# Layer input kept on chip between layers, with its squares summed in the output projection; paired heads in retention; a spare bank for the queries' sums

## What is computed

```python
def trunk_layer(x, c, pos, hist, norm_w, ada_w, ada_b, w_in, ...):
    mod = jax.nn.silu(c) @ ada_w + ada_b
    shift, scale, gate = jnp.split(mod[:, None, :], 3, axis=-1)
    h = rmsnorm(x, norm_w) * (1.0 + scale) + shift
    proj = h @ w_in                                  # 16 parts: q, k, v, gates of three branches
    ...
    o_ret = rmsnorm(o_r, ret_norm_w.reshape(H_RET, DV_RET)).reshape(B, S, BRANCH_W) * jax.nn.silu(rz)
    ...                                              # o_fox, o_gdn likewise
    q_g = l2norm(q_g.reshape(B, S, H_GDN, DK_GDN)) * (DK_GDN ** -0.5)
    br = jnp.einsum('bsnc,ncd->bsnd', jnp.stack([o_ret, o_fox, o_gdn], axis=2), w_branch)
    out = jnp.sum(br * jax.nn.sigmoid(mg), axis=2) @ w_out
    return x + gate * out, new_state
# after both layers: y = rmsnorm(x, final_norm_w)
```

## Time and profile before

| | |
|---|---|
| time, median of 3 runs | 3134.73 us (3130.49 to 3139.78) |
| the profiled execution's own time | 3135.03 us |
| span from its first to its last instruction | 3133.3 us |
| mean granted TensorE clock | 0.981 |
| TensorE busy | 2964.6 us, 95% |
| VectorE, ScalarE, GpSimd busy | 44%, 32%, 28% |
| traffic | 278.18 MB, 89 GB/s |

### The profile page before, as it was taken

The page is one execution under the profiler, slowest core; times in us unless marked ns, Lnnn a source line. Parts: engine busy times, 40 slices in busy tenths (PEclk is TensorE's granted clock), DMA queues, the critical chain, the costliest instruction groups (busy, mean ns, idle before and its releaser), DMA issues. The chain is left out here.

```text
span 3133.3 us, 52349 instructions
## 1 busy us (share of the span) xinstructions
PE 2964.6 (95%) x22200; PEld 2741.3 (87%) x22200; DVE 1365.4 (44%) x2813; ACT 997.5 (32%) x1798; POOL 890.0 (28%) x536
## 2 busy tenths in 40 slices
PE   7989999999999999999889999999999999999996
PEld 6889788879898989999888888878898989899995
DVE  4421555564536353245152325555636455333532
ACT  5122333333434343111051233333334333331201
POOL 1221122233434252332122122212425243333320
PEclk9999999999999999999999999999999999999998
DMA  6230222221212122333442312111212212133334
GB/s 236 96 111 30 70 77 77 77 67 55 60 56 73 40 64 102 124 124 101 178 138 86 109 71 73 68 56 56 85 44 77 62 59 57 43 134 123 123 100 169
DMA packets 127128, 278.18 MB, mean 89 GB/s; under 512 B 44912, under 2 KB 65008, under 8 KB 125872
## 3 DMA queue, kind: packets, MB, share of 16 engines
q1 hardware_dynamic: 126896, 274.83, 26.5%
HBM read 212.71 MB, written 57.60 MB: 86 GB/s over the span
## 5 line engine op out<-in xcount | busy, mean ns | idle before, releaser
L277 PE MATMUL ps<-sb_h_split,sb_w_split 128*128 128x364 f32 (+1 forms) x3456 | 1214.8, 352 | 28.6 <-ACT sb_fox L309 8.9
L278 PE MATMUL ps<-sb_h_split,sb_w_split 128*128 128x364 f32 (+1 forms) x3456 | 1144.8, 331 | 0.0
L279 PE MATMUL ps<-sb_h_split,sb_w_split 128*128 128x364 f32 (+1 forms) x3456 | 1144.1, 331 | 0.0
L277 PEld LDWEIGHTS ps<-sb_h_split,sb_w_split 128*128 128x128 f32 x3456 | 660.6, 191 | 62.0 <-issue 14.1
L278 PEld LDWEIGHTS ps<-sb_h_split,sb_w_split 128*128 128x128 f32 x3456 | 660.2, 191 | 6.3 <-issue 0.3
L279 PEld LDWEIGHTS ps<-sb_h_split,sb_w_split 128*128 128x128 f32 x3456 | 658.1, 190 | 0.0
L325 POOL CAST sb_w_split<-sb_w_raw 128x1024 fp32r<-128x1024 f32 x152 | 172.3, 1133 | 1637.5 <-PE ps L279 1575.3
L327 POOL TENSOR_TENSOR sb_w_split<-sb_w_raw,sb_w_split 128x1024 fp32r<-128x1024 f32 x152 | 378.2, 2488 | 12.2
L1207 ACT ACTIVATE sb_fox<-sb_fox 128x128 f32<-128x128 f32 (+5 forms) x144 | 112.0, 778 | 334.5 <-DVE sb_fox L1242 334.2
L279 PE MATMUL ps<-sb_o_split,sb_wb_split 128*128 128x364 f32 (+1 forms) x576 | 189.3, 329 | 0.0
L278 PE MATMUL ps<-sb_o_split,sb_wb_split 128*128 128x364 f32 (+1 forms) x576 | 189.0, 328 | 0.0
(11 more groups left out here) (244 smaller groups left out, 4097.0 us busy)
## 6 DMA issues: line engine op xcount, KB each, us to landing
sb_w_raw<-in_wblk SPq DMA_DIRECT2D x158, 512.0 KB, 3.8
scratch_gates<-sb_spill SPq DMA_DIRECT2D x72, 182.0 KB, 1.9
sb_o_split<-scratch_o SPq DMA_DIRECT2D x24, 544.0 KB, 5.9
sb_fox<-scratch_fcum SPq DMA_DIRECT2D x8, 1600.0 KB, 6.3
sb_w_raw<-in_wbr SPq DMA_DIRECT2D x48, 256.0 KB, 3.9
sb_raw_qk<-scratch_gates SPq DMA_DIRECT2D x22, 544.0 KB, 3.7
sb_w_raw<-in_adaw SPq DMA_DIRECT2D x20, 512.0 KB, 7.4
sb_ada<-in_adaw SPq DMA_DIRECT2D x16, 512.0 KB, 12.2
```

What stands on the lines that cost most here:

```text
L277: pe.matmul(out, w_hi, x_hi, start=first, stop=False)
L278: pe.matmul(out, w_hi, x_lo, start=False, stop=False)
L279: return pe.matmul(out, w_lo, x_hi, start=False, stop=last)
```

## The change

1. x stays in SBUF. `sb_x` and `sb_rstd` live from merge to the next norm phase; `mg` is the same memory as x. Once two merged slabs are split, SP loads two slabs of the old x over them, in four transfers, ahead of the last weight blocks. VectorE adds the projected output to x in place; x is still stored to `dx` (in layer 0 only).
2. In merge ScalarE squares each finished slab j into one of two spare slabs (into `extra` for j = 0); VectorE adds them up in `extra` from j = 2 on, one block behind; at the end TensorE sums `extra` and the last square over the partitions into banks 5 to 7, and ScalarE makes rstd by Ln and Exp, all ahead of the barrier. Layer 1's norm phase neither loads x nor squares nor sums. Layer 1's merge scales x and stores the result; `final_norm` is gone. The first two weight blocks of layer 1 are loaded in merge.
3. VectorE's order in both norm phases: `rows` of the next group stands ahead of `rest` of this one, `over_root` behind `columns`.
4. Retention: scores and the queries' outputs alternate between the two heads; the gate's transpose stands behind the first key transposes, in ring bank 1; ScalarE copies all outputs out and squares both heads before the first Ln. The fill is 96 turns before and after.
5. Delta groups: the third sum of the queries goes to SUM_BANK, without a wait. The wait for the spilled gates' stores stands at the end of the fourth group.

```diff
+def sum_features(pe, ring, n, sq, last_bank=None):
     for s, (a, w) in enumerate(SEGS):
-        ring.acquire(pe, n + s)
-        pe.matmul(ps[:, ring.bank(n + s), 0:w], ones, sq[:, a:a + w],
-                  start=True, stop=True).then_inc(*bank_ready.up(1))
+        bank = ring.bank(n + s)
+        if s == 2 and last_bank is not None:
+            bank = last_bank
+        else:
+            ring.acquire(pe, n + s)
+        pe.matmul(ps[:, bank, 0:w], ones, sq[:, a:a + w], start=True, stop=True).then_inc(*bank_ready.up(1))
...
+            for c in range(4):
+                sp.dma_start(x[:, 2 * c:2 * c + 2, :], A["xT"][2 * c:2 * c + 2].rearrange("k p t -> p k t"))\
+                    .then_inc(*branch_loaded[c].up(16))
...
-        dve.wait_ge(*inverse(1))
+        dve.wait_ge(*params_loaded(64))
+        rows(0)
+        columns(0)
+        if L == 0:
+            dve.wait_ge(*inverse(1))
         over_root(0)
         over_root(1)
-        dve.wait_ge(*params_loaded(64))
-        rows(0)
-        over_root(2)
-        columns(0)
-        over_root(3)
         for g in range(4):
+            if g < 3:
+                rows(g + 1)
             dve.wait_ge(*scaled(g + 1))
             rest(2 * g)
             rest(2 * g + 1)
             if g < 3:
-                rows(g + 1)
-                if g < 2:
-                    over_root(2 * g + 4)
                 columns(g + 1)
-                if g < 2:
-                    over_root(2 * g + 5)
+                over_root(2 * g + 2)
+                over_root(2 * g + 3)
...
-    OUT, NORM = [[13, 14, 15], [16, 20, 21]], [17, 22]
+    OUT, NORM = [[13, 15, 17], [14, 16, 18]], [19, 22]
...
-            ring.acquire(pe, 1 + n)
+            e = (0, 2, 3)[n]
+            ring.acquire(pe, e)
             for j in range(c):
-                mm = pe.transpose(ps[:, ring.bank(1 + n), P * j:P * j + P],
+                mm = pe.transpose(ps[:, ring.bank(e), P * j:P * j + P],
                                   Q4(k_)[:, t + j, :], ident)
             mm.then_inc(*bank_ready.up(1))
+            if n == 0:
+                pe.wait_ge(*gates_raw(1))
+                pe.transpose(ps[:, ring.bank(1), P:2 * P], mrow, ident).then_inc(*bank_ready.up(1))
             turns(fill, 4)
-        for h in range(2):
-            for n, (t, c) in enumerate(G3):
-                e = 4 + 3 * h + n
-                ring.acquire(pe, e)
-                for j in range(c):
-                    mm = pe.matmul(ps[:, ring.bank(e), P * j:P * j + P],
+        for n, (t, c) in enumerate(G3):
+            for h in range(2):
+                ring.acquire(pe, 4 + 2 * n + h)
+            for j in range(c):
+                for h in range(2):
+                    mm = pe.matmul(ps[:, ring.bank(4 + 2 * n + h), P * j:P * j + P],
                                    Q4(k_)[64 * h:64 * h + 64, t + j, :],
                                    Q4(q)[64 * h:64 * h + 64, t + j, :], start=True, stop=True)
-                mm.then_inc(*bank_ready.up(1))
-                turns(fill, 4)
+                    if j == c - 1:
+                        mm.then_inc(*bank_ready.up(1))
+            turns(fill, 8)
...
+        def outputs(n):
+            t, c = G3[n]
             pe.wait_ge(*state_ready(t + c - 1 if t < 8 else 8))
-            for tt in range(t, t + c):
-                mm = pe.matmul(ps[:, ring.bank(e), P * (tt - t):P * (tt - t) + P],
-                               V[:, tt, P * h:P * h + P], Q4(AT[h])[:, tt, :],
-                               start=(tt == t), stop=False)
+            for h in range(2):
+                e = OUT[h][n]
+                ring.acquire(pe, e)
+                for tt in range(t, t + c):
+                    pe.matmul(ps[:, ring.bank(e), P * (tt - t):P * (tt - t) + P],
+                              V[:, tt, P * h:P * h + P], Q4(AT[h])[:, tt, :],
+                              start=(tt == t), stop=False)
             for tt in range(max(t, 1), t + c):
-                mm = pe.matmul(ps[:, ring.bank(e), P * (tt - t):P * (tt - t) + P],
-                               S[64 * h:64 * h + 64, 9 if tt == 8 else tt, :],
-                               Q4(q)[64 * h:64 * h + 64, tt, :], start=False, stop=(tt == t + c - 1))
-            mm.then_inc(*bank_ready.up(1))
+                for h in range(2):
+                    mm = pe.matmul(ps[:, ring.bank(OUT[h][n]), P * (tt - t):P * (tt - t) + P],
+                                   S[64 * h:64 * h + 64, 9 if tt == 8 else tt, :],
+                                   Q4(q)[64 * h:64 * h + 64, tt, :], start=False, stop=(tt == t + c - 1))
+                    if tt == t + c - 1:
+                        mm.then_inc(*bank_ready.up(1))
...
+            outputs(n)
+            turns(fill, 10)
         pe.wait_ge(*squares(1))
         for s in range(3):
             norm_sum(0, s)
...
-            act.wait_ge(*act_took(3 if h == 0 else 9))
-            act.activation(sq, raw[h], ACT.Square).then_inc(*squares.up(1))
+            act.wait_ge(*act_took(5 + h))
+            act.activation(sq[h], raw[h], ACT.Square).then_inc(*squares.up(1))
         for m in range(6):
             taken(m)
         act.wait_ge(*normed(2))
         copy_out(0, 0)
+        copy_out(1, 0)
         taken(6)
         copy_out(0, 1)
+        copy_out(1, 1)
+        taken(7)
         copy_out(0, 2)
+        copy_out(1, 2)
         square(0)
-        taken(7)
-        copy_out(1, 0)
-        root(0, 0)
+        square(1)
         taken(8)
-        root(0, 1)
-        root(0, 2)
-        invert(0, 0, TOK, 7)
         taken(9)
-        copy_out(1, 1)
+        for s in range(3):
+            root(0, s)
+        invert(0, 0, TOK, 9)
         taken(10)
-        copy_out(1, 2)
-        square(1)
         taken(11)
...
-        sum_features(pe, ring, 3, sq[0])
+        sum_features(pe, ring, 3, sq[0], SUM_BANK)
...
+                bank = SUM_BANK if x == 0 and s == 2 else ring.bank(first + s)
+                act.activation(rt[x][:, a:a + w], ps[:, bank, 0:w], ACT.Ln,
...
-def merge(L, ph):
+def merge(L, x, rstd, ph):
     NU = 24
-    work = ph.enter_context(nc.sbuf_tensor(f"sb_merged_{L}", [P, KC * TOK + TOK], F32))
-    mg = work[:, 0:KC * TOK].rearrange("p (k t) -> p k t", k=KC)
+    mg = x
...
+    extra = ph.enter_context(nc.sbuf_tensor(f"sb_gate_{L}", [P, TOK], F32))[:, :]
...
+        pe.wait_ge(*squares_used(KC - 2))
+        for s, (a, w) in enumerate(SEGS):
+            pe.matmul(ps[:, 5 + s, 0:w], ones, extra[:, a:a + w], start=True, stop=False)
+        pe.wait_ge(*squares(KC))
+        for s, (a, w) in enumerate(SEGS):
+            pe.matmul(ps[:, 5 + s, 0:w], ones, spare[1][:, a:a + w], start=False, stop=True)\
+                .then_inc(*norm_sums.up(1))
+    @block.sync
+    def _(sp):
+        source = A["xT"] if L == 0 else dx
+        for c in range(4):
+            sp.wait_ge(*normed(2 * c + 2))
+            sp.dma_start(x[:, 2 * c:2 * c + 2, :], source[2 * c:2 * c + 2].rearrange("k p t -> p k t"))\
+                .then_inc(*tile_loaded[c].up(16))
+        for b in range(40, LATE):
+            late_follow(sp, L, b)
+        if L == DEPTH - 1:
+            sp.dma_start(nwT[:, :], A["fnwT"]).then_inc(*params_loaded.up(16))
+            for k in range(KC):
+                sp.wait_ge(*out_done(k + 1))
+                sp.dma_start(O["yT"][k], x[:, k, :]).then_inc(*stored.up(16))
+            sp.wait_ge(*stored(16 * KC))
+            return
+        for n in range(2):
+            sp.dma_start(wraw[:, 4 + n], row("wblk", (L + 1) * N_BLOCKS + n)).then_inc(*params_loaded.up(16))
+        for j in range(KC):
+            sp.wait_ge(*dve_took(3 * (j + 1)))
+            sp.dma_start(dx[j], x[:, j, :]).then_inc(*stored.up(16))
+            if j == 5:
+                sp.wait_ge(*split_ready(LATE - 2))
+                for n in range(4):
+                    sp.dma_start(wraw[:, n], row("adaw", L * 24 + 24 + (0, 1, KC, KC + 1)[n]))\
+                        .then_inc(*params_loaded.up(16))
+        sp.wait_ge(*stored(16 * KC))
+        sp.wait_ge(*params_loaded(96))
...
+        for j in range(KC):
+            act.wait_ge(*dve_took(3 * (j + 1)))
+            if j > 2:
+                act.wait_ge(*squares_used(j - 2))
+            act.activation(spare[j % 2] if j else extra, x[:, j, :], ACT.Square).then_inc(*squares.up(1))
+        for s, (a, w) in enumerate(SEGS):
+            act.wait_ge(*norm_sums(s + 1))
+            act.activation(rstd[:, a:a + w], ps[:, 5 + s, 0:w], ACT.Ln, bias=eps_c,
+                           scale=1.0 / D).then_inc(*roots.up(1))
+        act.wait_ge(*roots(3))
+        act.activation(rstd[:, :], rstd[:, :], ACT.Exp, scale=-0.5).then_inc(*inverse.up(1))
...
-                    ins = dve.scalar_tensor_tensor(spare[j % 3][:, a + b:a + b + n],
+                    ins = dve.scalar_tensor_tensor(x[:, j, a + b:a + b + n],
...
+            if j > 1:
+                dve.wait_ge(*squares(j))
```

(12 more changed lines are left out.)

220 lines of the change are left out of this document (67 added, 153 removed).

## The result

The changed kernel takes 3062.03 us (median of 4 runs, 3052.57 to 3066.76) against 3134.03 before: a ratio of 0.976 (95% interval 0.9738 to 0.9782), 72 us less. Forecast were 3056, in a range of 3040 to 3080. Run again beside the experiments it took 3057.15 (3056.03 to 3064.72) against 3135.05, ratio 0.976 (0.9747 to 0.9773). The profiled run after took 3066.76 us (span 3065.0), the longest of its four, so its span is 68.3 shorter than before, not 72. Its runs lie up to 14 us apart; the experiments show one piece of that spread, not all of it.

The account below looks back on a forecast made before the run. The prediction took TensorE, busy 2964.6 of 3133.3 us, as the bound. Gains of 23 (end), 0 (join and norm phases together), 25 (retention) and 31 (delta groups) made 79 off 3134.7: 3056 us, range 3040 to 3080.

Parts of the forecast that it names:

- Part 1: End of the run: last scaling starts 8.1 us after x's last update, about 23 us off, bounds 20 to 24.
- rival (e): Output projection: VectorE becomes the bound, waiting for ScalarE's square while the next block waits for VectorE; 3152 us, 1%.
- Part 2: Join of the layers: earlier rstd and modulation let layer 1's first projection start at about 1571, 15 us earlier.
- the split's share: Join: GpSimd's third weight split slows VectorE's remainders by 0 to 2.2 us; half was taken, 1.1.
- Part 3: Norm phases: VectorE's new order loses 5.3 us per layer in groups 1 and 2, about 0.5 more at group 3.
- Part 4: Retention groups: two heads overlap in different array rows for scores and queries' outputs; about 25 us off, bounds 3 to 27.
- The six switches of 0.1: Retention: six switches between array shapes disappear, counted at 0.1 us each, though no row prices one.
- Part 5: Delta groups: queries' third sum no longer waits; 22.9 us of stop and 8.5 of half clock saved, about 31, bounds 20 to 33.
- (a): Retention: heads in turn do not overlap, only the switches go; gain 3 us instead of 25, 3078 us, 8%.
- (b): Delta groups: the stop moves to the fill at line 277 and the clock still falls; gain 4 instead of 31, 3083, 8%.
- (c): Norm phases: new order worse than summed, every stop cold and the split in the way; 10 us lost, 3066, 15%.
- (d): Norm phases: new order costs nothing because something else holds TensorE there; 10 us better, 3046, 15%.

Follow-up runs that it names:

- run alone, the parts: Three kernels, against the kernel before: x on chip with the new norm order 3121.03 us, retention groups 3109.45 us, queries' third sum in the spare bank 3105.56 us.
- the second profile: Profiled execution of the changed kernel run again, unedited: 3056.03 us, in a series with median 3057.15 us against 3135.05 for the kernel before.

## Why the prediction was right, and where it was not

The time fell inside the range, 6 us above the forecast in one series and 1 in the other, and the likeliest case was the one that came. That it came so near is luck in part: run alone, the parts gave 14.4, 29.2 and 29.5 where 23, 25 and 31 were forecast, and errors of both signs cancel in the sum. The bounds of 3045 to 3068, said to follow from the parts' own bounds, do not: those add up to 3042 to 3102. The parts, in their order:

- **Part 1, the end: right, with one wrong term.** 23.0 against 23. The scaling starts 8.3 us behind the last update. The six sums were put at 3.6 "at that rate", but a quarter of 17.47 is 4.4; they took 3.9 (3043.47 to 3047.40) at a granted clock of 1.00, where the 24 of before ran at 0.85 on the mean. In the second profile the scaling starts later: the six sums take 5.6 at a mean clock of 0.72 and the end gives 21.3, between the bounds of 20 and 24. The Exp starts 0.01 behind its table load of 1.28, so the dearer switch of the Trainium skill, "ScalarE: Activation LUTs", section What ACT_TABLE_LOAD costs, is not on this path. The work put into the output projection cost nothing that the stretch shows: VectorE's add took 1.28 to 1.58 within its idle time, the blocks still follow one another at 12.0 us, and rival (e) is out.
- **Part 2, the join: 11.1 instead of 12.9.** The step that was too small is the landing of the modulation weights. I took 5.0 us from four blocks that had the queue to themselves; here ten blocks were issued in a row (five of the modulation, a weight block, four more of the modulation), with a median of 6.6 us to landing for the first five, and the second modulation started 20.5 us behind the update of x, where 18 were forecast. And the split's share, of which I took half, fell due in full: the remainders took 4.99 us in layer 1 and 5.62 in layer 0, where 2.86 are usual. The rule of "SBUF — State Buffer", section Who interferes with whom, in the Trainium skill was right against my half, in both layers.
- **Part 3, the norm phases: right in size and place.** 7.1 and 8.0 lost against 7.8; TensorE waits 2.48 behind the low half in groups 1 and 2. Undoing the order gives them back (71.4 and 69.4 us).
- **Part 4, retention: the mechanism was right, the sum was not.** Heads overlap (2.8 for scores, 2.6 for outputs; 2.9 and 2.7 forecast). The late Ln cost 0.9 in the first group of a layer (0.8 forecast); in the second it cost nothing at once, but 0.75 at the first fill of the attention. Two terms failed. The six switches of 0.1, which no run prices, are inside these differences already: 2.4 us counted twice. And "the stop at the gates shrinks by 0.3" took a stop for a constant that the profile of before showed at 3.2, 3.6, 4.1 and 7.6 in four groups of one kind. That spread was the sign that something beside the group sets its length, and the prediction passed over it. In the first profile it cost 4.5 us in layer 1; in the second it gave back 0.3, and retention gave 23.9 in all, against 25.
- **Part 5, the delta groups: right.** 31.6 against 31. Fill matmuls follow one another at 0.30 us at half clock and at 0.17 at full; behind the sums of the five groups that had half clock this comes to some 7.5 us, and leaves some 24 for the stop itself.
- **Rivals.** (a) is out by the records of the scores, (b) by the clock of 1.00 and the missing wait, (c) and (d) by the marks, (e) by the blocks' 12 us. None of them named what moved retention in layer 1: the stop at the key transposes.
